# Branch projections, mixing gates and output projection of a hybrid SSM/attention layer: eight block products or seven

## The reference, cut to what matters

```python
y_ssm = y @ w_ssm_branch                    # 512x2048 by 2048x1024
y_att = o.reshape(bsz, s, D_ATT) @ w_attn_branch   # 512x1024 by 1024x1024
g_ssm, g_att = jnp.split(jax.nn.sigmoid(mix_g), 2, axis=-1)   # mix_g: 2048 columns of h @ w_in
mixed = g_ssm * y_ssm + g_att * y_att
x = x + mixed @ w_o                         # 512x1024 by 1024x1024
h = rms_norm(x, g_norm_mlp)
x = x + jnp.square(jax.nn.relu(h @ w_up)) @ w_down
```

## Time and profile before

| | before |
|---|---|
| median of three runs | 1266.85 us (1265.89 to 1267.10) |
| profiled execution, first to last instruction (its span) | 1265.3 us |
| the runs' median above that span | 1.55 us |
| TensorE busy | 1244.3 us, 98%, 6716 matmuls |
| VectorE busy | 765.2 us, 60% |
| ScalarE busy | 581.4 us, 46% |
| GpSimd busy | 405.1 us, 32% |

### The profile page before, as it was taken

One profiled execution on the slowest core, in us unless ns is written; L12 is line 12 of the kernel. 1 busy time (PEld: TensorE's weight loads), 2 busy tenths in 40 slices (PEclk: granted clock), 3 DMA queues, 4 the chain that ended last, 5 costly groups with the idle time before them and its releaser, 6 DMA issues.

```text
span 1265.3 us, 19135 instructions
## 1 busy us (share of the span) xinstructions
PE 1244.3 (98%) x6716; PEld 1024.2 (81%) x6716; DVE 765.2 (60%) x1352; ACT 581.4 (46%) x1012; POOL 405.1 (32%) x271
## 2 busy tenths in 40 slices
PE   9999999999999999999999999999999999999997
PEld 7888877777888888888888888888878888888885
DVE  6945887775577877787864111111048848479487
ACT  6315466666544554354443222222266346254364
POOL 3433355545333333333334444444430110301200
PEclk9999999999999999999999999999999999999999
DMA  8533410000232222232222333334352061440601
GB/s 245 157 90 60 88 37 2 1 2 2 67 83 68 69 80 66 66 83 67 76 73 84 94 91 99 99 99 137 133 186 92 22 213 31 132 133 17 211 5 66
DMA packets 170327, 108.39 MB, mean 86 GB/s; under 512 B 25284, under 2 KB 161830, under 8 KB 170278
## 3 DMA queue, kind: packets, MB, share of 16 engines
q1 hardware_dynamic: 170038, 107.65, 29.1%
q10 hardware_dynamic: 240, 0.09, 0.0%
HBM read 104.84 MB, written 2.10 MB: 85 GB/s over the span
## 4 chain that ended last, share of the span: by engine, by line
PE 87%; DVE 5%; ACT 4%; issue 2%; POOL 1%; DMA 1%; SPq 0%; DVEq 0%; ACTq 0%; POOLq 0%
PE bank L2460 21%; PE bank L2055 16%; PE bank L2469 10%; PE bank L2564 8%; PE bank L2059 8%; PE bank L2569 4%; PE bank L2303 2%; PE bank L2479 2%; PE bank L2243 2%; PE bank L2282 2%; POOL prob L865 1%; PE bank L2104 1%; PE bank L2485 1%; PE bank L2440 1%; PE bank L2143 1%
## 5 line engine op out<-in xcount | busy, mean ns | idle before, releaser
L845 POOL TENSOR_TENSOR wlo<-raw,whi 128x1024 fp32r<-128x1024 f32 x133 | 323.2, 2430 | 693.8 <-ACT whi L1091 388.5
L1091 ACT ACTIVATE whi<-raw 128x1024 fp32r<-128x1024 f32 x96 | 101.7, 1060 | 295.6 <-PE bank L2469 160.0
L2055 PE MATMUL bank<-h_hi,whi 128*128 128x512 f32 x456 | 181.6, 398 | 0.7 <-DVE h_lo L1332 0.7
L2055 PE MATMUL bank<-h_lo,whi 128*128 128x512 f32 x456 | 177.9, 390 | 0.0
L2460 PE MATMUL bank<-h_hi,whi 128*128 128x512 f32 x384 | 150.3, 391 | 1.3 <-DVE grp L1775 0.7
L2460 PE MATMUL bank<-h_lo,whi 128*128 128x512 f32 x384 | 149.4, 389 | 0.0
L2059 PE MATMUL bank<-h_hi,wlo 128*128 128x512 f32 x456 | 112.9, 390 | 0.0
L1863 DVE TENSOR_TENSOR mt<-bank,sig 128x512 f32<-128x512 f32 x16 | 11.1, 691 | 161.6 <-PE bank L2469 161.6
L1755 DVE SCALAR_TENSOR_TENSOR grp<-bank,vt,grp 128x511 f32<-128x511 f32 (+2 forms) x96 | 71.8, 748 | 58.9 <-ACT grp L1115 49.9
L865 POOL TENSOR_SCALAR prob<-prob,rsum,gate 128x512 f32<-128x512 f32 (+3 forms) x128 | 79.4, 635 | 80.4 <-DVE rsum L1599 80.4
L2055 PEld LDWEIGHTS bank<-h_hi,whi 128*128 128x128 f32 x456 | 85.7, 188 | 20.1 <-DVE h_lo L1332 2.5
(11 more groups left out here) (321 smaller groups left out, 2548.4 us busy)
## 6 DMA issues: line engine op xcount, KB each, us to landing
raw<-in_w_in SPq DMA_DIRECT2D x71, 512.0 KB, 3.8
raw<-in_w_up SPq DMA_DIRECT2D x32, 512.0 KB, 4.0
draw<-in_w_down SPq DMA_DIRECT2D x16, 1024.0 KB, 6.5
raw<-in_w_ssm_branch SPq DMA_DIRECT2D x16, 512.0 KB, 3.6
raw<-in_w_in SPq DMA_DIRECT2D x28, 256.0 KB, 3.4
raw<-in_w_attn_branch SPq DMA_DIRECT2D x8, 512.0 KB, 3.6
raw<-in_w_o SPq DMA_DIRECT2D x8, 512.0 KB, 3.7
x_sb<-in_x SPq DMA_DIRECT2D x4, 512.0 KB, 5.4
```

Of the source, the lines that this page charges most:

```text
L845: nc.gpsimd.tensor_tensor(wlo[slot][:], raw[slot][:], whi[slot][:].bitcast(F32), ALU.subtract).then_inc(wlo_ready, units)
L1091: nc.scalar.activation(whi[slot][:], raw[slot][:], ACT.Copy).then_inc(whi_ready, 1)
L2055: T.matmul(bank[slot][:], whi[slot][:, k * P:(k + 1) * P], part[:, k, :], start=(k == 0 and n == 0), stop=False)
```

## The change

The six products become six *whole* products, done one after the other (`whole`, `G` = 0 to 5: o, y's first half, y's second half, the gate of the attention branch, the gate of the SSM branch, the output), each token-major as the output product was, and each by seven block products instead of eight. Left and right operands are cut in 2 x 2 blocks: left blocks A11 to A22 of 512 features by 256 tokens, weight quadrants "11" to "22" of 512x512. With the sums S1 = A21 + A22, S2 = S1 - A11, S3 = A11 - A21, S4 = A12 - S2 on the left and T1 = 12 - 11, T2 = 22 - T1, T3 = 22 - 12, T4 = 21 - T2 on the right (the diff makes T2 as T3 + 11 and T1 as 22 - T2) the seven block products are A11 x 11, A12 x 21, S2 x T2, S1 x T1, S3 x T3, S4 x 22 and A22 x T4. Their results are added up in PSUM where that can be and otherwise by VectorE (`c_add`) and by copies of ScalarE (`c_copy`).

- SP loads weight quadrants in halves of 256 rows by 512 columns (512 KB). The first product's eight halves come during the SSM groups, one per group.
- A weight half (128x1024) is split by ScalarE (`q_high`) and GpSimd (`part_low`), 14 halves per product, in a ring of three pairs of tiles. VectorE makes the T sums (`t_sum`, eight operations of 128x1024 per product); in the first product GpSimd makes four of them.
- o and y are kept as single float32 tiles, no longer as two parts; their blocks and the S sums are split before use, by ScalarE (`left_high`) and VectorE (`left_low`), 128x1024 each. The S sums of h are made from its high and low parts (`h_sum`) and used by both gate products.
- The gates are sigmoids over whole quadrants (two 128x512 tiles at a time), the gated products and their sum are made per quadrant (`o_gate`, `mixed_sum`), and TensorE turns each quadrant of the sum with eight transposes (`turn_m`), 32 in all.
- The banks of PSUM are taken in pairs, so that copies and additions read 128 x 2 x 512.
- The norm behind the output product takes token tiles 2 and 3 first, then 0 and 1.
- `o_lo`, `y_hi`, `y_lo` and the old units of mixing and output product fall away. The MLP keeps its work; its semaphores are shared with the new products.

```diff
--- before.py
+++ after.py
...
+        ORDER = [("11", "21", "T2", "T1", "T3", "22", "T4")] * 4
+        ORDER += [("11", "21", "T2", "22", "T1", "T3", "T4"), ("11", "21", "T4", "T2", "T1", "T3", "22")]
+        LEFT_OF = {"11": "A11", "21": "A12", "T2": "S2", "T1": "S1", "T3": "S3", "22": "S4", "T4": "A22"}
+        SUMS = [("T3", "T2", "T1", "T4")] * 5 + [("T3", "T2", "T4", "T1")]
...
+        def part_slot(G, n, part):
+
+            at_part = 14 * G + n
+            if at_part == 0:
+                return twos((first_hi, first_lo)[part][:])
+            return twos(([whi[0], wlo[0]], [whi[1], wlo[1]], third)[(at_part - 1) % 3][part][:])
...
+            HALVES = [(name, h) for name in ("11", "12", "22", "21") for h in range(2)]
+            for after in range(1, GROUPS):
+                ssm_load(after, 2)
+                if after == 1:
+                    sp.wait_ge(o_ready, PAIRS // 2)
+                quad_half(0, *HALVES[after - 1])
+                for j in range(3, 6):
                     ssm_load(after, j)
...
+            def part_low(G, n):
+
+                pool.wait_ge(q_hi, 14 * G + n + 1)
+                nc.gpsimd.tensor_tensor(part_slot(G, n, 1), part_at(G, n), part_slot(G, n, 0).bitcast(F32),
+                                        ALU.subtract).then_inc(q_lo, 1)
+
+            part_low(0, 0)
+            pool.wait_ge(wlo_ready, U_MLP)
+            for name in ("22", "12"):
+                pool.wait_ge(quad_loaded[name], 32)
+            for h in range(2):
+                rows = slice(2 * h, 2 * h + 2)
+                nc.gpsimd.tensor_tensor(quad(0, "T3")[:, rows], quad(0, "22")[:, rows], quad(0, "12")[:, rows],
+                                        ALU.subtract).then_inc(q_sums, 1)
+            part_low(0, 1)
+            for h in range(2):
+                rows = slice(2 * h, 2 * h + 2)
+                pool.wait_ge(q_lo, h + 1)
+                pool.wait_ge(q_sums, h + 1)
+                nc.gpsimd.tensor_tensor(quad(0, "T2")[:, rows], quad(0, "T3")[:, rows], quad(0, "11")[:, rows],
+                                        ALU.add).then_inc(q_sums, 1)
+            for n in range(2, 14):
+                part_low(0, n)
+            for G in range(1, 6):
+                for n in range(14):
+                    part_low(G, n)
             with pool.Fori(0, 4) as q:
...
+            def q_high(G, n):
+
+                name, at_part = ORDER[G][n // 2], 14 * G + n
+                if name[0] == "T":
+                    act.wait_ge(q_sums, sums(G, name, n % 2))
+                else:
+                    act.wait_ge(quad_loaded[name], 32 * (G + 1))
+                if at_part in (1, 2):
+                    act.wait_ge(unit_done, U_MLP - 2 + at_part)
+                elif at_part == 3:
+                    act.wait_ge(yd_done, 2 * GROUPS)
+                elif at_part:
+                    act.wait_ge(part_done, at_part - 2)
+                nc.scalar.activation(part_slot(G, n, 0), part_at(G, n), ACT.Copy).then_inc(q_hi, 1)
+
...
+            left_high(0, "A12")
+            q_high(0, 3)
+            left_high(0, "S2")
+            squares(GROUPS - 1)
+            left_high(0, "S1")
+            for h in range(2, 14):
+                q_high(*divmod(h + 2, 14))
+                if h in (2, 6, 8, 10):
+                    c_copy(0, ORDER[0][h // 2 - 1])
+                if h in (4, 6, 7):
+                    left_high(0, {4: "S3", 6: "S4", 7: "A22"}[h])
+                if h in (9, 11):
+                    left_high(1, {9: "A11", 11: "A12"}[h])
+            for G in (1, 2):
+                for h in range(14):
...
+            def t_sum(G, name, h):
+
+                rows = slice(2 * h, 2 * h + 2)
+                if name == "T3":
+                    for source in ("22", "12"):
+                        dve.wait_ge(quad_loaded[source], 32 * (G + 1))
+                    dve.wait_ge(q_lo, lows(G - 1, "T4", 1))
+                    x, y2, op = quad(G, "22"), quad(G, "12"), ALU.subtract
+                elif name == "T2":
+                    dve.wait_ge(q_lo, lows(G, "11", h))
+                    dve.wait_ge(q_sums, sums(G, "T3", h))
+                    x, y2, op = quad(G, "T3"), quad(G, "11"), ALU.add
+                else:
+                    dve.wait_ge(q_sums, sums(G, "T2", h if G else 1))
+                    if name == "T4":
+                        dve.wait_ge(q_lo, lows(G, "21", h))
+                    x, y2, op = quad(G, "22" if name == "T1" else "21"), quad(G, "T2"), ALU.subtract
+                V.tensor_tensor(quad(G, name)[:, rows], x[:, rows], y2[:, rows], op).then_inc(q_sums, 1)
+
...
+                to = sum_place(3, name)
+                if name in ("S1", "S3"):
+                    x, y2, op = ("A21", "A22", ALU.add) if name == "S1" else ("A11", "A21", ALU.subtract)
+                    step(V.tensor_tensor(to[:], block_of(0, x), block_of(0, y2), op))
+                    step.wait()
+                    step(V.tensor_tensor(to[:], to[:], block_of(1, x), ALU.add))
+                    step.wait()
+                    ins = V.tensor_tensor(to[:], to[:], block_of(1, y2), op)
...
+            def left_low(G, name):
+
+                dve.wait_ge(lhi_ready, left_count(G, name))
+                slot = LEFT_SLOT[G][name]
+                if G == 0 and name == "S1":
+                    dve.wait_ge(yms_done, GROUPS)
+                source = sum_place(G, name)[:] if name[0] == "S" else left_source(G, name)
+                V.tensor_tensor(left_lo[slot][:], source, left_hi[slot][:].bitcast(F32), ALU.subtract).then_inc(llo_ready, 1)
...
+            def c_add(G, name, q):
+
+                dve.wait_ge(part_done, parts(G, name))
+                if COPIES[G]:
+                    dve.wait_ge(c_copied, copies_to(G, name))
+                if adds_to(G, name, q) > 1:
+                    dve.wait_ge(c_added, adds_to(G, name, q) - 1)
+                to = product_to(G, q)
+                V.tensor_tensor(to, bank_pair[PAIR_AT[G][name][0]][:], to, ALU.add).then_inc(c_added, 1)
...
+            def o_gate(q):
+
+                dve.wait_ge(gate_sig, GATE_ORDER[0].index(q) + 1)
+                V.tensor_tensor(o_prod[:, q], o_prod[:, q], mixing[:, q], ALU.mult).then_inc(o_gated, 1)
+
+            def mixed_sum(q):
+
+                dve.wait_ge(gate_sig, 4 + GATE_ORDER[1].index(q) + 1)
+                step(V.tensor_tensor(y_prod[:, q], y_prod[:, q], mixing[:, q], ALU.mult))
+                step.wait()
+                V.tensor_tensor(y_prod[:, q], y_prod[:, q], o_prod[:, q], ALU.add).then_inc(o_gated, 1)
...
+            left_low(0, "A12")
+            s_sum(0, "S1")
+            s_sum(0, "S2")
             steps.n, steps.base = 0, GROUPS * 6 - 4
             gated(GROUPS - 1)
+            left_low(0, "S2")
             sum_squares(GROUPS - 1)
-            norm_root(GROUPS - 1, sums=6)
-            normed_y(GROUPS - 1, spread=6)
-            low_y(GROUPS - 1)
-            with dve.Fori(0, 4) as m:
-                for t in range(2):
-
-                    dve.wait_ge(mix_sig, m * 4 + (2 * t + 2))
-                    dve.wait_ge(mlo_ready, m * 2 + (t + 2))
-                    for i, done in ((1, 3), (0, 5)):
-                        dve.wait_ge(unit_done, m * 10 + (U_MIX + 5 * t + done))
-                        V.tensor_tensor(mt[:, i, :], bank[4 * t + 3 - i][:], sig[:, i, :], ALU.mult).then_inc(mix_part, 1)
-                    dve.wait_ge(mix_part, m * 4 + (2 * t + 2))
-                    V.tensor_tensor(mt[:, 0, :], mt[:, 0, :], mt[:, 1, :], ALU.add).then_inc(mix_sum, 1)
-                    where = bass.ds(m * 2 + t, 1)
-                    dve.wait_ge(mhi_ready, m * 2 + (t + 1))
-                    V.tensor_tensor(m_lo[:, where, :], mt[:, 0:1, :], m_hi[:, where, :].bitcast(F32),
-                                    ALU.subtract).then_inc(mlo_ready, 1)
-
-
-            dve.sem_inc(down_added, 4)
-
...
+                def high(n, t):
+                    for kl in range(2):
+                        for part in (hi, lo):
+                            T.matmul(banks[:, t, :], part[:, 2 * (n % 2) + kl, t * P:(t + 1) * P], part_slot(G, n, 0)[:, kl, :],
+                                     start=(fresh and n % 2 == 0 and kl == 0 and part is hi), stop=False, skip_group_check=True)
+
+                def low(n, t):
+                    for kl in range(2):
+                        mm = T.matmul(banks[:, t, :], hi[:, 2 * (n % 2) + kl, t * P:(t + 1) * P], part_slot(G, n, 1)[:, kl, :],
+                                      start=False, stop=(n % 2 == 1 and kl == 1), skip_group_check=True)
                     return mm
 
...
+                for n in (2 * p, 2 * p + 1):
+                    pe.wait_ge(q_hi, 14 * G + n + 1)
+                    if 14 * G + n == 83:
+                        pe.wait_ge(q_lo, 14 * G + n + 1)
+                        for t in range(2):
+                            high(n, t)
+                            low(n, t).then_inc(part_done, 1)
```

(38 more changed lines are left out.)

752 lines of the change are left out of this document (523 added, 229 removed), and 4 rows, old and new, of the table LEFT_SLOT.

## The result

| | before | after |
|---|---|---|
| median of the runs on one chip | 1266.89 us (4 runs) | 1349.07 us (4 runs, 1347.29 to 1350.78) |
| ratio to before, 95% interval | | 1.0651 (1.0637 to 1.0664) |
| profiled execution, its span | 1265.3 us | 1345.5 us |
| end of GpSimd's last low part of the six products | | 997.67 us |
| TensorE's first matmul of the MLP | 928.2 us | 1009.3 us |

The change costs 82.2 us (1349.07 - 1266.89), and 81.1 of them have been lost when the MLP begins (1009.3 - 928.2, in the profiled executions).

What follows compares the result with a forecast made beforehand. TensorE bounds the kernel before; after the change, GpSimd and VectorE taking turns bound the stage. 55.9 us of turns + 27 idle - 1 for the norm = +82 on the 1265.3 span, 1347, plus 1.55: 1349 us; range 1318 to 1388.

Steps and rivals of the forecast that it cites:

- The turns: Changed stage: GpSimd subtractions and VectorE operations on two SBUF tensors never run side by side; a pair costs 3.34 us.
- 114 VectorE operations: Six products: VectorE's new 128x1024 operations with two SBUF inputs, 114 in all, 130.0 us back to back.
- The sum over the stage: Six products: 88 pairs 293.9 us, 26 left-over VectorE operations 29.6, decay products 2.6: 326.1 us, before idle time.
- From when: Stage start: turn-taking begins at 649.4 us, after GpSimd's last SSM unit; without idle time its last low part ends at 975.5.
- The four decay products: Last SSM group: these VectorE operations now meet GpSimd too, adding 4 x 0.65 = 2.6 us.
- Both idle, 27 us: Six products: waits with GpSimd and VectorE both idle, 7, 1.5, 7, 1.5 and 10 us, sum 27.
- TensorE's gain: Changed stage: seven block products for eight, 235.8 us against 264.4, 28.6 us less if TensorE stays the bound.
- The first rival: Changed stage: new collisions cost nothing, TensorE stays the bound, some 8 us of waits: 1246 us; chance 0.09.
- TensorE at the lower clock: Changed stage: TensorE, idle a third of it, falls to half the clock: 1467 us, or between; chance 0.04.
- The signs: Changed stage if right: TensorE's share near 70%, its waits released by low parts, stage about 355 us.
- Costed at nothing: Dropped o and y copies (0 to 5.7 us gain, taken 0), ScalarE's work and SP's loads, all taken as hidden.
- The norm: Behind the output product: keeps its chain of 8.9 us, two token tiles come early, 1 us less.

Runs made afterwards that it cites:

- seventh run: Changed kernel with GpSimd's low parts of the six products left out, the low tiles filled with zeros in 28 pieces, nothing read from SBUF: 1246.98 us.
- the second: Changed kernel with 13 left block sums written to two empty PSUM banks, so 21 VectorE operations have one input from PSUM: 1338.18 us.
- the third run: Changed kernel with all 84 low parts of the six products made by VectorE instead of GpSimd: 1312.32 us.
- the fourth: Changed kernel with three extra unread TensorE matmuls ahead of each half unit in products two to four: 1347.76 us.

## Why the prediction was right, step by step

**The turns.** Right, in mechanism and in price: a pair costs 3.29 us against 3.34, and the T sums came to 2.43 us, the low parts to 3.03. The count of 114 VectorE operations is met by the trace. In its wording the claim was too narrow: VectorE's copies and scalings of a single tensor take turns too.

**The sum over the stage.** Its terms sorted by product (pairs, left-over operations, idle time), beside the lengths of the windows above (the last to 997.67):

| product | 1 | 2 | 3 | 4 | 5 | 6 | sum |
|---|---|---|---|---|---|---|---|
| predicted, us | 73.1 | 54.0 | 62.9 | 52.8 | 49.0 | 61.3 | 353.1 |
| measured, us | 78.6 | 54.9 | 57.5 | 56.1 | 49.7 | 61.0 | 357.8 |

**From when.** Wrong. The low part at 646.98 us in the earlier trace rows was not the last of the SSM stage: it was the first unit's of the mixing loop, made 4.28 us after GpSimd's last SSM unit had ended at 642.7. So in the changed kernel the turns begin at 639.87, 9.5 us sooner than I had them: 6.7 for the wrong unit, 2.8 because the SSM stage itself came out shorter. There they run beside SSM operations of VectorE that the sum did not hold. The four decay products took 10.66 us in the record, GpSimd's turns among them, in the place of 2.60. GpSimd's last low part ended at 997.67, where 975.5 + 27 is 1002.5: the longer stage (4.7) makes up for half of the earlier start (9.5). The decay product's matmuls:

```profile
659.09 3.68 PE L2910 MATMUL bank<-mdec,xdt 128*64 128x128 f32 x32 [5.50 <-DVE mdec L2079]
```

They begin at 659.1, near the forecast (658.5), though the turns had begun sooner than it said.

**Both idle, 27 us.** The term was nearly twice too large as worded. From the intervals of both engines in the timeline, neither is at work for 14.8 of the 357.8 us. The length of the stage came out nearly right because VectorE also worked alone: in the first product the two together cover 73.9 us, GpSimd 48.9, so that VectorE had 25.0 without it. In the third product I had let seven us pass for eight additions from PSUM; GpSimd's next low parts ran beside them, and it came out 5.4 us shorter.

**TensorE's gain.** 28.6 us were forecast if it stayed the bound. The seventh run shows 19.9 (1266.88 - 1246.98); a part of the difference is the first product, where TensorE is busy for 54.66 of the 60 us from 640 to 700. The first rival's 1246 is within 1 us of that run. It priced a kernel without turns well, but so close a match is in part luck: it held 8 us of waits by estimate, and GpSimd's part took 1.85 us in that run, not 2.41. So the ledger is about -20 for TensorE's work and +102 for GpSimd's reading subtractions, most of it turns by the estimate above.

**TensorE at the lower clock.** I gave it 0.04 and said that a granted clock below 1.00 would speak against the forecast. As a sign that was wrong: the clock fell, and the forecast held. Timeline and two windows of the changed kernel around a wait:

```profile
702.65 0.80 PE L2969 MATMUL bank<-third,left_hi 128*128 128x512 f32 x1 [3.95 <-ACT third L1275]
...
704.52 0.63 PE L2969 MATMUL bank<-third,left_hi 128*128 128x512 f32 x1
704.95 0.63 PE L2969 MATMUL bank<-third,left_lo 128*128 128x512 f32 x1
...
707.93 0.39 PE L2969 MATMUL bank<-whi,left_hi 128*128 128x512 f32 x1
708.16 0.39 PE L2969 MATMUL bank<-whi,left_lo 128*128 128x512 f32 x1
```

```profile
702.00:706.00 4.00, 3.35 (x8) 2.67 (x9) 4.00 (x2) 4.00 (x5) 3.33 (x2) 0.50 0.00 0
...
710.00:714.00 4.00, 4.00 (x19) 3.34 (x18) 4.00 (x3) 2.54 (x4) 4.00 (x2) 1.00 1.03 383
```

After 3.95 us of idle time the matmuls start 0.43 us apart (704.52 to 704.95) at a granted clock of 0.50, the 1.2 GHz level, and 0.23 apart soon after. The Trainium skill, "TensorE: Matmul & The Clock Gate", section "HAM oscillation — how this bites in real kernels", describes such falls; the trace agrees that they happen. Nothing shows that they set the time, as the rival had it: the second and the third run are shorter at about the same clock, and the fourth at a higher one is not. One place where the lower clock shows is the norm: 24 transposes took 3.02 us before and 4.49 in the changed kernel, at a mean granted clock of 0.62.

```profile
1005.06 4.49 PE L3035 MATMUL bank<-cst,xn 128*128 128x128 f32 x24 [2.78 <-ACT xn L1475]
```

**The signs.** Two that I named were off. TensorE's share of the stage is 281.1 of 357.8 us, 79% and not 70. Its matmuls are longer at the lower clock, and the last SSM group's rest lies in it; how much each adds is not shown. And its waits are mostly ended by VectorE's additions and splits, 4.4 us only by the low parts: it is VectorE's order that TensorE meets first.

**Costed at nothing.** The copies that fall away, SP's loads and ScalarE's work were to move nothing by more than a few us. GpSimd's last SSM unit ended 2.8 us sooner (639.9 and 642.7), and the span from the MLP's first matmul on is 336.2 us in place of 337.1; both agree with that. The norm does not. From the last matmul of the output product to the MLP's first it took 8.5 us (1000.8 to 1009.3) where it was 5.6 (922.6 to 928.2), and the forecast had 1 us less than before. In it TensorE waits 2.78 us for ScalarE's scaled rows, and then come the slower transposes above.

**The last digit.** That 1349 meets 1349.07 is luck. The product stage ended 4.4 us sooner than forecast (1000.8 and 1005.2), the norm took 3.9 us more, and the median lies 3.6 us above the profiled span where I added 1.55, as the profiled execution was the fastest of the four (1347.29). The mechanism and the size of the loss were foreseen; the parts are off by 2 to 12 us and cancel.

## What to carry to other kernels

Before work is moved from a full engine to two free ones, ask whether these two can work at the same time. Here TensorE's relief was worth 20 us, and GpSimd and VectorE, both less than half busy in the stage before, cost 102 us with subtractions that read SBUF, most of it (by estimate) because their operations exclude each other. Look for an overlap of just this kind of pair in the profile (a duration that ends one operation's time after the other engine's end), price it, and count pairs; then put one input of VectorE's operation in PSUM, or give the whole work to the faster of the two. Both helped here, and neither was enough to beat the kernel before.

## What the runs showed of the hardware that was not expected

- GpSimd's subtraction of two tensors takes 2.30 us for 128x1024, its copy of one 1.09 us in the attention stage; in turns with VectorE a pair with the copy costs 1.99 us (23.9 for twelve), one with the subtraction 3.29.
- VectorE writing to PSUM from two SBUF tensors takes turns (3.19 us each in the profile's mean): an output in PSUM does not exempt it, an input does.
- A shorter VectorE operation does not make the pair cheap: with 128x512 it costs 33.15 / 12 = 2.76 us.
- 28 small fills by GpSimd took 1.85 us, about 0.07 us each from start to start, about half of the 0.13 us that a single one shows as its duration.
